# Pads of 32 bytes between the buffers of an fp32 network's matmul operands

## What is computed

```
x = layer_norm(x)
for l in 0, 1:                      # first block
    x = layer_norm(alpha*x + hybrid_mixer(x, w_in[l], w_branch[l], w_mix_out[l]))
    x = layer_norm(alpha*x + cross_attention(x, mem, xa_q[l], xa_kv[l], xa_o[l]))
    x = layer_norm(alpha*x + conv_ffn(x, ffn_w_in[l], ffn_w_out[l]))      # 2816 wide
for l in 0, 1:                      # second block
    x = x + g1 * mixer_2(rmsnorm(x)*(1+sc1)+sh1)
    h = rmsnorm(x)*(1+sc2)+sh2
    x = x + g2 * (swiglu(h) if l == 0 else moe_swiglu(h))                 # 3584 wide, 8 experts
return rmsnorm(x)
```

## Time and profile before

| | |
|---|---|
| median of three runs | 2803.29 us |
| profiled execution, own time | 2804.18 us |
| its span | 2802.4 us |
| TensorE matmul busy | 2721.5 us, 97% |
| TensorE weight loads busy | 2499.1 us, 89% |
| VectorE busy | 2108.0 us, 75% |
| ScalarE busy | 1693.9 us, 60% |
| matmuls | 18410 |
| granted TensorE clock, mean | 0.987 |

### The profile page before, as it was taken

How to read it: one execution, slowest core, us unless ns; L and a number is a source line. 1 busy time by engine, 2 the same in 40 slices (tenths; PEclk the granted TensorE clock), 3 DMA queues, 4 the chain that set the end, 5 groups by cost and what they waited for, 6 DMA issues and landing times.

```text
span 2802.4 us, 42816 instructions
## 1 busy us (share of the span) xinstructions
PE 2721.5 (97%) x18410; PEld 2499.1 (89%) x18418; DVE 2108.0 (75%) x2088; ACT 1693.9 (60%) x1856; POOL 71.8 (3%) x114
## 2 busy tenths in 40 slices
PE   7999999999999999999999999999999999999998
PEld 6999999999999989989999999888888888888886
DVE  5777647876667658767577667688898989888896
ACT  4555536654555546645577654677777777677675
POOL 1100000001000000000000000000000000000000
PEclk9999999999999999999999989999999999999999
DMA  7545447745536457634588733698988989898894
GB/s 237 170 147 166 154 159 257 268 141 170 157 121 196 151 181 268 229 96 136 187 296 299 256 93 106 244 371 339 379 340 339 377 344 372 335 382 338 340 373 182
DMA packets 304403, 679.22 MB, mean 242 GB/s; under 512 B 16560, under 2 KB 238032, under 8 KB 261072
## 3 DMA queue, kind: packets, MB, share of 16 engines
q1 hardware_dynamic: 288832, 617.67, 61.5%
q0 software_dynamic: 15376, 58.75, 6.4%
HBM read 675.32 MB, written 4.69 MB: 243 GB/s over the span
## 4 chain that ended last, share of the span: by engine, by line
PE 79%; DVE 10%; ACT 8%; issue 2%; DMA 1%; SPq 0%; ACTq 0%; DVEq 0%
PE bank L550 75%; DVE ew_lo L1871 4%; ACT ring_tail L2058 3%; ACT w_hi L1989 2%; DVE ring_low L1362 1%; PE bank L1166 1%; DMA ring_head<-in_w_in 1%; PE bank L630 1%; DVE std L1295 1%; PE bank L590 1%; DVE ring_tail L1319 0%; DVE ring_low L1282 0%; PE bank L669 0%; DVE xT L1616 0%; ACT ew_hi L2342 0%
## 5 line engine op out<-in xcount | busy, mean ns | idle before, releaser
L1871 DVE TENSOR_TENSOR ew_lo<-ring_head,ew_hi 128x2048 fp32r<-128x2048 f32 x336 | 759.3, 2287 | 41.5 <-ACT ew_hi L2342 41.5
L2342 ACT CAST ew_hi<-ring_head 128x2048 fp32r<-128x2048 f32 x336 | 640.6, 1915 | 223.9 <-PE bank L550 223.8
L550 PE MATMUL bank<-xs_hi,ring_low 128*128 128x256 f32 (+1 forms) x2608 | 511.9, 283 | 0.0
L550 PEld LDWEIGHTS bank<-xs_hi,ring_low 128*128 128x128 f32 (+1 forms) x2608 | 414.1, 190 | 1.5 <-issue 0.7
L550 PE MATMUL bank<-ew_hi,xe_hi 128*128 128x512 f32 x896 | 353.2, 394 | 0.0
L550 PE MATMUL bank<-ew_hi,xe_lo 128*128 128x512 f32 x896 | 349.3, 390 | 0.0
L550 PE MATMUL bank<-ew_lo,xe_hi 128*128 128x512 f32 x896 | 348.7, 389 | 0.0
L550 PE MATMUL bank<-x_hi,w_hi 128*128 128x256 f32 x1152 | 322.0, 287 | 13.5 <-ACT x_hi L2050 7.7
L550 PE MATMUL bank<-x_hi,ring_low 128*128 128x256 f32 x1152 | 316.6, 281 | 0.0
L1362 DVE TENSOR_TENSOR ring_low<-ring_head,w_hi 128x2048 fp32r<-128x2048 f32 x105 | 240.0, 2289 | 101.1 <-ACT w_hi L1989 101.1
L550 PE MATMUL bank<-x_lo,w_hi 128*128 128x256 f32 x1080 | 296.9, 281 | 0.0
(11 more groups left out here) (430 smaller groups left out, 5497.7 us busy)
## 6 DMA issues: line engine op xcount, KB each, us to landing
ring_head<-in_moe_w_gate SPq DMA_DIRECT2D x112, 1024.0 KB, 7.2
ring_head<-in_moe_w_up SPq DMA_DIRECT2D x112, 1024.0 KB, 7.0
ring_head<-in_moe_w_down SPq DMA_DIRECT2D x112, 1024.0 KB, 7.1
ring_head<-in_w_in SPq DMA_DIRECT2D x82, 1024.0 KB, 5.4
ring_tail<-in_ada_w POOLq DMA_DIRECT2D x48, 1024.0 KB, 10.0
ring_head<-in_ffn_w_in SPq DMA_DIRECT2D x44, 1024.0 KB, 6.4
ring_head<-in_ffn_w_out SPq DMA_DIRECT2D x22, 1024.0 KB, 8.7
ring_head<-in_xa_kv SPq DMA_DIRECT2D x16, 1024.0 KB, 5.4
```

The lines of the kernel that those rows point to most:

```text
L550: ins = nc.tensor.matmul(out, lhsT, rhs, start=start, stop=stop, **kw)
L1871: v.tensor_tensor(ew_lo[:, h, :], ring(c % 6), ew_hi[:, h, :].bitcast(F32), ALU.subtract).then_inc(w_used[c % 6], 1)
L2342: a.copy(ew_hi[:, (e * len(PARTS) + c) % DEPTH_HI, :], ring(c % 6)).then_inc(f.count(part_hi), 1)
```

## The change

Pads of 8 fp32 values (32 bytes in each partition; one of 16 values, 64 bytes) are declared between the buffers. Nothing reads or writes them. No instruction, wait, transfer or order is changed; the start addresses of the tensors behind a pad move: by 32 bytes for `chunk_high`, by 64 for the mixer's tensors and the splits that lie behind `ring_tail`, by 96 for `w_hi`, 128 for `x_*` and `act_*`, and 32 for `xe_*` and `eact_*`. `ew_hi` and `ew_lo` stay where they were, and so do `ring_low`, `ring_head`, `xs_*` and `ring_tail`.

```diff
--- before.py
+++ after.py
@@ -42,6 +42,7 @@
 MIXER_CHUNKS = 16
 NARROW = 40
 DT_AT = 32
+SKEW = 8
 class Follow:
 
 
@@ -204,8 +205,10 @@
         with ExitStack() as loads:
             with ExitStack() as twin:
                 xs = [in_scope(twin, n, KD, TOK, dt=F32R) for n in ("xs_hi", "xs_lo")]
+                skew_chunk = in_scope(twin, "skew_chunk", SKEW)
                 chunk_high = in_scope(twin, "chunk_high", CH, dt=F32R)
             ring_tail = in_scope(loads, "ring_tail", SLOTS - 6, CH)
+            skew_loads = in_scope(loads, "skew_loads", 2 * SKEW)
             with ExitStack() as twin:
                 _, qb_hi, qb_lo, _, hc_hi, hc_lo, qa_hi, qa_lo = (in_scope(twin, n, k, TOK, dt=F32R) for n, k in (
                     ("under_q", 12), ("qb_hi", 4), ("qb_lo", 4), ("under_v", 12), ("hc_hi", 4), ("hc_lo", 4), ("qa_hi", 4), ("qa_lo", 4)))
@@ -220,10 +223,13 @@
                 qhalf = [[in_scope(mixer, f"qhalf{a}{m}", 4, TOK) for m in range(2)] for a in range(2)]
                 probsT = in_scope(mixer, "probsT", 2, 2, 2, TOK)
             with ExitStack() as ffns:
+                skew_high = in_scope(ffns, "skew_high", SKEW)
                 w_hi = in_scope(ffns, "w_hi", DEPTH_HI, CH, dt=F32R)
+                skew_x = in_scope(ffns, "skew_x", SKEW)
                 x_hi, x_lo = (in_scope(ffns, n, KD, TOK, dt=F32R) for n in ("x_hi", "x_lo"))
                 act_hi, act_lo = (in_scope(ffns, n, 2, 2, TOK, dt=F32R) for n in ("act_hi", "act_lo"))
         ew_hi, ew_lo = (sb(n, DEPTH_HI, CH, dt=F32R) for n in ("ew_hi", "ew_lo"))
+        skew_xe = sb("skew_xe", SKEW)
         xe_hi, xe_lo = (sb(n, KD, P, dt=F32R) for n in ("xe_hi", "xe_lo"))
         eact_hi, eact_lo = (sb(n, ETILES, P, dt=F32R) for n in ("eact_hi", "eact_lo"))
```

## The result

The change makes the kernel slower. Its median is 2830.6 us against 2804.5 us for the kernel before on the same chip, a ratio of 1.009 with a 95% interval of 1.0079 to 1.0102: 26 us more, where 17 less were forecast. The profiled execution took 2835.4 us.

The account below looks back on a forecast made before the run. TensorE's matmul pace was taken to bound the kernel; gains of 11.9 us (experts), 3.7 (feed-forward) and 1.8 (chunks), together 17.4, took 2804.2 to 2786.8 profiled, 2785.9 by the median. Forecast 2786 us, range 2782 to 2798.

Parts of the forecast that it names:

- What bounds the kernel: Whole kernel: TensorE, busy for 97% of 2802.4 us, sets the time by the pace at which matmuls follow each other.
- Offsets modulo 64 as the variable: Matmuls: operands' start addresses modulo 64 set the pace; 256 columns take 120.0 ns if alike, 116.7 if different.
- (0, 32): Stationary and moving operand's starts modulo 64, sought for most products; 116.7 ns at 256 columns, but 117.8 at 1320 us.
- (32, 0): Turned chunks: stationary operand starts 32 past a multiple of 64, moving at 0; 118.5 ns at 256 columns, credited zero.
- Carrying the 8 cycles from 256 to 512 columns: Experts' 512-column matmuls: the 3.3 ns saved at 256 columns was taken to hold there too, 3584 matmuls, 11.9 us gained.
- The bounds: Per 512-column expert matmul: a loss of 3.3 ns, 0, or a gain of 1.6 or 3.3 ns.
- The slower rival: Experts: `xe` behind `ew` falls on the next 8-cycle step, losing 11.9 us against 5.5 gained elsewhere; 2809.7 us, chance 0.06.
- The experts' structure: Experts: 64 of 504 matmuls at each of seven changeovers gain nothing, as TensorE waits there; transfers still feed the stage.
- The 14-step block at nothing: Feed-forward with 14 steps, 1392 to 1620 us: no gain, its 17.7 us period being set by ScalarE and VectorE.
- The feed-forward's 3.7 us: Feed-forward of the two first layers: 1536 matmuls x 1.1 ns and 48 x 3.3 ns, twice, 3.7 us gained.
- The chunks' 1.8 us: Chunks with `chunk_high`: 2016 matmuls x 1.1 ns, 2.2 us, taken as 1.8 us gained.
- The rule of two ports: Rule against the forecast, for all matmuls: two independent SBUF read ports, so addresses can't matter and the sum is 0.

Follow-up runs that it names:

- the sweep: A kernel computing nothing of the reference, TensorE alone running 48-matmul stretches at set distances from stationary to moving operand; 512 columns: 226.9 ns at 0, 233.2 at 224.
- e5: Kernel before, with pads putting unturned 256-column products of projections and feed-forward at distance 32, experts left at 0: 2806.4 us against 2805.7, ratio 1.0004.
- e3: Kernel before plus all pads of the change but the one ahead of `xe_hi`: 2810.9 us, ratio 1.002.
- e6: Kernel before, with pads putting unturned 256-column products of projections and feed-forward at distance 192, experts left at 0: 2787.0 us, ratio 0.9942.

## Why the prediction was wrong, step by step

- **What bounds the kernel**: right. The time is the pace of TensorE's matmuls, VectorE's and ScalarE's operations stayed equal, and the whole difference is in the pace.
- **Offsets modulo 64 as the variable**: wrong, and the first step that failed. All pairs that I called (0, 32) before lay at a distance of exactly 32 bytes modulo 256, so the earlier trace rows could not tell "different modulo 64" from "32 apart". After the change the products are spread over 32, 96, 160 and 224. `x` against `ring_low` went from 32 to 160, where the sweep has 120.0 ns; that is why the feed-forward lost 1.1 ns instead of gaining 1.1, although the pairs with `w_hi` did come to 32. The last down step, the one product with `w_hi` alone, fell from 120.0 to 117.8 ns, 2.2 of the 3.3 ns forecast (the second pace of the row at 1320 us), and so confirmed the reading for the case it was taken from and nothing more. The alternative was in my own text, as a bound: (32, 0) at 118.5 ns is distance 224, and the sweep gives 118.4.
- **Carrying the 8 cycles from 256 to 512 columns**: wrong, and the costly one. It rested on both having 32 cycles over their columns at distance 0. But 0 is the worst for 256 columns or near it, and the best for 512: 119.9 against 226.9 ns, and then at 32 117.8 against 233.3. An excess that belonged to the load of the weights would have moved both alike. The sweep's 512-column row at 224 has 233.2 ns, 560 cycles, the 72 of the expert 16.79 us. I had named this as the step on which most hangs and as one that no row shows, and still gave it more than half of the chance.
- **The bounds**: the loss was bounded at 3.3 ns, "the same 8 cycles the other way". It was 6.1 ns, 15 cycles. A symmetric bound about an unknown mechanism was no bound; the rows had none to give.
- **The slower rival**: right in place and direction (the step above, `xe` behind `ew`), too small in size. It reckoned 11.9 us of loss in the experts and 5.5 of gain in the rest; the runs show 21 of loss and 6 of loss.
- **The experts' structure**: right. The stretch at a change of experts takes 0.4 of each expert's loss, the six ring slots fed a stage that never waited, and 504 less 64 matmuls an expert is the count that fits.
- **The 14-step block at nothing**: right, 10.6 us behind before it and 10.2 behind after it.
- **The feed-forward's 3.7 us**: wrong twice. The change did not bring the pace, and e5, which did, shows that the pace alone would not have brought the time. The prediction named no cover for it and did not ask what is late next; the earlier trace rows had the answer half in sight, VectorE busy for 145 and ScalarE for 116 of 182 us.
- **The chunks' 1.8 us**: not gained. With `chunk_high` `xs` went from 0 to 224 (119.9 to 118.4 ns in the sweep), but `mem`, `qa`, `qb`, `hc` and `out` went from 32 to 96 with `ring_low` (117.8 to 120.0). e3, which has these products as the changed kernel has them, starts the first cast into `w_hi` 0.2 us later than the kernel before, behind a whole layer's chunks, where some of the 1.8 us should have shown; no run takes them by themselves.
- **The rule of two ports** ("TensorE: Matmul & The Clock Gate", Part 2, step 1, in the Trainium skill) says that the next weights are read through a port of their own and take nothing from the running matmul; I had read it as saying that addresses can't matter. With TensorE alone at work the same 48 matmuls take between 5.45 and 5.76 us at 256 columns by nothing but the distance, so the measurement decides against that reading; whether it is the two reads that meet, no run here shows. It is no defence against my error either, since it would have said no change.

## What to carry to other kernels

Where a tuned kernel is bound by the pace of fp32r matmuls, take the distance between stationary and moving operand modulo 256 bytes as a parameter, and measure it for each number of columns with TensorE alone; here that table led to 19 us, some 4 of which may be the clock's. Two classes seen in a trace do not name the variable that separates them: list every variable on which they differ, and ask which values the change will visit that no row has. And where one engine is busy for 100% of a stage, measure how far behind the next one is before crediting a faster pace.

## What the runs showed of the hardware that I had not expected

- Four bytes can decide: at 512 columns 248 gives 230.0 ns and 244 gives 239.9; at 256 columns 112 gives 114.1 and 116 gives 121.9.
- One distance can have two paces, each held for a whole stretch: 113.3 or 117.8 ns at 192, 116.7 or 117.8 at 32.
- The excess exists only at the full clock. At 1.2 GHz the intervals are 213.3 ns, 256 cycles for 256 columns with nothing over, at a distance of 32 (after, e5) as at 192 (e6). The last down step of e5, three matmuls from one `act_lo` to the next:

```profile
610.46 0.42 PE L554 MATMUL bank<-act_lo,w_hi 128*128 128x256 f32 x1
...
613.03 0.41 PE L554 MATMUL bank<-act_lo,w_hi 128*128 128x256 f32 x1
```

2.57 us for 12 matmuls, 214 ns by the rounded starts. At the full clock 256 columns are 106.7 ns, and 6.6 to 15.2 ns come on top. So the excess is not a fixed number of clock cycles; what it is, no run took apart.
